# A two-layer streaming encoder on one core: stores of split weight tiles moved from the sync engine's queue to ScalarE's, with six edits of the step order around them

## The reference, cut to what matters

```python
def trunk(x, c, sample):
    for i in range(DEPTH):                                   # DEPTH = 2
        shift, scale, gate = modulation(c, ada_w[i], ada_b[i])        # silu(c) @ (1024 x 3072) + b
        h = rms_norm(x, norm_g[i]) * (1 + scale[:, None]) + shift[:, None]
        if i % 2 == 0:      # pool_mixer: u, gate = split(h @ w_in); trailing means of 2, 4, 8, 16 rows minus u;
            y, st = pool_mixer(h, hist, hist_pos, pool_w_in[j], pool_w_grp[j], pool_scale[j], pool_w_out[j])
        else:               # 16 heads on 4 key/value heads, chunk band of 3 x 64 keys, ALiBi, sink logits, silu gate
            y, kw, vw = attn_prompt(h, attn_w_in[j], attn_sinks[j], attn_w_out[j])   # attn_sample for the sample
        x = x + gate[:, None] * y
    return rms_norm(x, final_g), ...states
```

## Time and profile before

| what | us |
|---|---|
| runs, median (lowest to highest of 3) | 1622.16 (1614.68 to 1626.26) |
| profiled execution | 1625.29 |
| its span, first to last instruction | 1623.5 |
| TensorE busy in the span | 1565.5 |
| ScalarE busy in the span | 727.8 |
| mean granted TensorE clock | 0.984 of full |

### The profile page before, as it was taken

How to read it: one execution, slowest core, us unless ns; L and a number is a source line. 1 busy time by engine, 2 the same in 40 slices (tenths; PEclk the granted TensorE clock), 3 DMA queues, 4 the chain that set the end, 5 groups by cost and what they waited for, 6 DMA issues and landing times.

```text
span 1623.5 us, 26106 instructions
## 1 busy us (share of the span) xinstructions
PE 1565.5 (96%) x9211; PEld 1331.6 (82%) x9211; DVE 883.8 (54%) x2203; ACT 727.8 (45%) x1616; POOL 429.5 (26%) x403
## 2 busy tenths in 40 slices
PE   6899999999999999999999899999999999999997
PEld 4799988788878878788888898888788887888886
DVE  3465435563556455626666634666446664366652
ACT  3344433333332333225555554666435665456643
POOL 1233431211221212212222341333213333123332
PEclk9899999999999999999999999999999999999999
DMA  9688799996899699942233365334463334643323
GB/s 329 206 287 270 242 314 312 317 356 238 300 328 354 224 327 330 348 157 105 105 105 105 117 247 186 133 136 175 155 207 131 130 130 166 214 166 134 132 79 130
DMA packets 167855, 341.96 MB, mean 211 GB/s; under 512 B 22127, under 2 KB 84927, under 8 KB 167470
## 3 DMA queue, kind: packets, MB, share of 16 engines
q1 hardware_dynamic: 167726, 340.29, 60.0%
HBM read 266.13 MB, written 74.31 MB: 210 GB/s over the span
## 4 chain that ended last, share of the span: by engine, by line
PE 80%; DVE 6%; ACT 4%; issue 4%; DMA 2%; POOL 1%; SPq 0%; DVEq 0%; POOLq 0%; ACTq 0%
PE ps_u L1013 63%; PE ps_o L1258 4%; PE ps_s L1212 3%; PE ps_t L1231 3%; DMA work<-in_x_prompt_dram 1%; PE ps_s L1013 1%; DVE ps_u L1439 1%; PE ps_o L1057 1%; DMA w_raw<-in_pool_w_out_dram 1%; ACT ps_u L1760 1%; DVE work L1584 1%; DVE h_all_lo L1396 1%; ACT work L1865 1%; ACT sq L1806 1%; DVE silu_g L1468 1%
## 5 line engine op out<-in xcount | busy, mean ns | idle before, releaser
L1013 PE MATMUL ps_u<-h_all_hi,w_hi 128*128 128x512 f32 (+2 forms) x1440 | 520.6, 362 | 9.9 <-DVE h_all_lo L1396 2.9
L1013 PE MATMUL ps_u<-h_all_hi,w_lo 128*128 128x512 f32 (+2 forms) x1440 | 512.2, 356 | 0.0
L1013 PE MATMUL ps_u<-h_all_lo,w_hi 128*128 128x512 f32 (+2 forms) x1440 | 511.9, 355 | 0.0
L1013 PEld LDWEIGHTS ps_u<-h_all_hi,w_hi 128*128 128x128 f32 x1440 | 275.6, 191 | 55.4 <-DVE silu_g L1468 6.4
L1013 PEld LDWEIGHTS ps_u<-h_all_hi,w_lo 128*128 128x128 f32 x1440 | 275.9, 192 | 36.9
L1013 PEld LDWEIGHTS ps_u<-h_all_lo,w_hi 128*128 128x128 f32 x1440 | 276.0, 192 | 35.4
L2007 POOL TENSOR_TENSOR work<-work,recip 128x512 f32<-128x512 f32 (+2 forms) x136 | 133.0, 998 | 342.1 <-DVE recip L1601 340.6
L1013 PE MATMUL ps_u<-y_hi,w_hi 128*128 128x512 f32 (+1 forms) x584 | 214.6, 367 | 5.4 <-POOL y_lo L1986 5.3
L1439 DVE TENSOR_TENSOR ps_u<-ps_u,rstd_b 128x512 f32<-128x512 f32 (+1 forms) x180 | 107.1, 595 | 205.2 <-PE ps_u L1013 205.0
L1013 PE MATMUL ps_u<-y_hi,w_lo 128*128 128x512 f32 (+1 forms) x584 | 209.5, 359 | 0.0
L1013 PE MATMUL ps_u<-y_lo,w_hi 128*128 128x512 f32 (+1 forms) x584 | 209.2, 358 | 0.0
(11 more groups left out here) (240 smaller groups left out, 2321.5 us busy)
## 6 DMA issues: line engine op xcount, KB each, us to landing
w_hi<-w_hi_kept SPq DMA_DIRECT2D x176, 512.0 KB, 4.1
w_lo<-w_lo_kept SPq DMA_DIRECT2D x176, 512.0 KB, 5.4
chunks<-in_ada_w_dram SPq DMA_DIRECT2D x32, 512.0 KB, 6.3
w_hi_kept<-w_hi SPq DMA_DIRECT2D x28, 512.0 KB, 3.4
w_lo_kept<-w_lo SPq DMA_DIRECT2D x28, 512.0 KB, 4.8
w_hi_kept<-fore_hi SPq DMA_DIRECT2D x24, 512.0 KB, 6.4
w_lo_kept<-fore_raw SPq DMA_DIRECT2D x24, 512.0 KB, 7.8
opening<-in_ada_w_dram SPq DMA_DIRECT2D x16, 512.0 KB, 8.8
```

Source lines behind the costliest of these rows:

```text
L1013: last = nc.tensor.matmul(out, w, x, start=(i == 0), stop=(i == n - 1))
```

## The change

Seven edits, in the order of the steps:

1. The opening makes `h` in two halves. New steps `HF` make the second column block (272 columns) first; `W` 1 comes right behind them; `HS` of stage 0 makes the first block (272 columns) after the sums of squares. `XS` of x row tiles 0 and 1 moves up to their `XT`. The first two units wait for `HF` (new semaphores `h_first_hi`, `h_first_lo`), the third for `HS`.
2. GpSimd's `w_lo` of tile 2 waits until `SH` is done.
3. `XL` of the next part's row tiles 0 and 1 moves from the beginning of the output phase to before the last group's `z` units.
4. `MT` of modulation blocks 3 to 5 is cut into 6, 6 and 4 matmuls (`MP`, `MP`, `MT`), behind output tiles 5, 6 and 7 in place of all 16 behind tile 4.
5. In attention parts 1 to 3 the last item's `drain` moves from behind row block 6 of the first output unit to between row blocks 3 and 4 of the fourth.
6. In attention part 0 the first drained slot uses the ordinary order of its steps (softmax ahead of the low half of the turned weights).
7. `keep_tile` moves from the sync engine to ScalarE. ScalarE's step `W` of tile j, after its copy to `w_hi`, waits for both halves of tile j-1 and asks for its two stores; at the last tile of the stage it also waits for and stores that one.

```diff
             for t in range(n_tok):
                 s.append(("XT", 0, t))
+                if t < 2:
+                    s.append(("XS", 0, t))
                 if t == 1:
                     s.append(("MT", 0))
+            s.extend([("HF", k) for k in range(KT)])
+            self.split_to(1)
+            s.extend([("XS", 0, t) for t in range(2, n_tok)])
+            s.append(("NA", 0, 0))
             s.extend([("HS", 0, k) for k in range(KT)])
-            self.split_to(1)
-            s.extend([("XS", 0, t) for t in range(n_tok)])
-            s.append(("NA", 0, 0))
...
+            if g == GROUPS - 1 and p + 1 < PARTS:
+                s.extend([("XL", p + 1, 0), ("XL", p + 1, 1)])
             j = self.tile(("grp", g))
...
-            begin = [[("XL", p + 1, 0), ("XL", p + 1, 1)]]
+            begin = []
...
-            behind[4] = behind.get(4, []) + [("MT", 2 + p)] + ([("SH", 1)] if p == 2 else [])
+            m = 2 + p
+            behind[5] = behind.get(5, []) + [("MP", m, 0, 3)]
+            behind[6] = behind.get(6, []) + [("MP", m, 3, 6)]
+            behind[7] = behind.get(7, []) + [("MT", m)] + ([("SH", 1)] if p == 2 else [])
...
-        drain = [slot(a, drained=p == 0) for a in tail + [None, None, None]]
-        plan = [(0, 0, 6), drain[0], (1, 0, 6), drain[1], (2, 0, 6), drain[2], (3, 0, 6)]
+        drain = [slot(a, drained=p == 0 and a != tail[0]) for a in tail + [None, None, None]]
+        plan = [(0, 0, 6), drain[0], (1, 0, 6), drain[1], (2, 0, 6), drain[2]]
         if p == 0:
-            plan += [drain[3], (4, 0, 6)]
-        plan += [(0, 6, 7), drain[-1], (1, 6, 7), (2, 6, 7), (3, 6, 7)]
+            plan += [(3, 0, 6), drain[3], (4, 0, 6), (0, 6, 7), drain[-1]]
+        else:
+            plan += [(3, 0, 4), drain[-1], (3, 4, 6), (0, 6, 7)]
+        plan += [(1, 6, 7), (2, 6, 7), (3, 6, 7)]
...
                 elif st[0] == "W":
-                    keep_tile(st[1])
...
-                            if u["u"] not in stage_first:
+                            if u["u"] == 0:
+                                pe.wait_ge(h_first_hi, k + 1)
+                                pe.wait_ge(h_first_lo, k + 1)
+                            elif u["u"] not in stage_first and u["u"] != 2:
                                 pass
...
+                elif kind == "HF":
...
+                    for c, w, v in spans(COLS // 2, COLS // 2):
+                        last = V.scalar_tensor_tensor(out=h_lo[:, k, c:c + w], in0=x_even[:, k, c:c + w], scalar=gain[:, 0, k, v:v + 1],
+                                                      in1=h_hi[:, k, c:c + w].bitcast(F32), op0=ALU.mult, op1=ALU.subtract)
+                    last.then_inc(h_first_lo, 1)
...
         @block.scalar
         def _(act):
             A = nc.scalar.activation
+            owned = [st[1] for st in steps if st[0] == "W"]
+
+            def keep_tile(j):
+
+                act.wait_ge(w_hi_ready, splits(j))
+                act.wait_ge(w_lo_ready, splits(j))
+                n, i = width[j], kept.index(j)
+                act.dma_start(w_hi_dram[i, :, 0:n], w_hi[:, slot_of[j], 0:n].bitcast(F32)).then_inc(w_kept[slot_of[j]], 16)
+                act.dma_start(w_lo_dram[i, :, 0:n], w_lo[:, slot_of[j], 0:n].bitcast(F32)).then_inc(w_kept[slot_of[j]], 16)
...
                     A(w_hi[:, slot_of[j], 0:width[j]], w_raw[:, slot_of[j], 0:width[j]], ACT.Copy).then_inc(w_hi_ready, 1)
+                    if j - 1 in owned:
+                        keep_tile(j - 1)
+                    if j + 1 not in owned:
+                        keep_tile(j)
...
+                elif kind == "HF":
...
+                    for c, w, v in spans(COLS // 2, COLS // 2):
+                        last = A(h_hi[:, k, c:c + w], x_even[:, k, c:c + w], ACT.Copy, scale=gain[:, 0, k, v:v + 1])
+                    last.then_inc(h_first_hi, 1)
...
-                    for c, w, v in spans(0, cols(p)):
+                    for c, w, v in spans(0, cols(p) if stage else COLS // 2):
...
+                    if j == 2:
+                        pool.wait_ge(shift_ready, 1)
                     pool.wait_ge(w_hi_ready, splits(j))
```

More of the change, by code:

```diff
@@ L571, in trunk_kernel @@
         h_hi_ready, h_lo_ready = sem("h_hi_ready"), sem("h_lo_ready")
+        h_first_hi, h_first_lo = sem("h_first_hi"), sem("h_first_lo")
         ssum_done, var_ready, rstd_ready, diag_ready, rstd_spread, rb_ready = (
@@ L834, in load_tile @@
                 load_raw(t, w_raw[:, slot_of[j], :], raw_loaded[slot_of[j]])
[L836 to L842, removed]
             def fetch_tile(j):
@@ L912, in _ @@
                         load_ada(i + CHUNKS - 1)
-                elif st[0] == "W":
-                    keep_tile(st[1])
                 elif st[0] == "WL":
@@ L1047, in _ @@
                     last.then_inc(ada_done, 1)
-                elif kind == "MT":
+                elif kind in ("MP", "MT"):
                     m = st[1]
-                    if m >= 1:
+                    if kind == "MP" and st[2] == 0 or kind == "MT" and 1 <= m < 3:
                         claim("o", (mod_ready, m + 1))
@@ L1054, in _ @@
                         pe.wait_ge(ada_added, KT * (m + 1) - summed_from)
-                        for k in range(KT):
+                        for k in range(*st[2:4]) if kind == "MP" else range(6, KT):
                             for v in range(2):
@@ L1058, in _ @@
                                                         ones[:, 0:1], start=True, stop=True)
-                        last.then_inc(mod_turned, 1)
+                        if kind == "MT":
+                            last.then_inc(mod_turned, 1)
                         continue
@@ L1384, in _ @@
                         last.then_inc(x_put_dve, 1)
+                elif kind == "HF":
+                    k = st[1]
+                    dve.wait_ge(h_first_hi, k + 1)
+                    if k == 0:
+                        dve.wait_ge(x_put_dve, xt_dve[(0, TILES - 1)])
+                        dve.wait_ge(x_put_act, xt_act[(0, TILES)])
+                    for c, w, v in spans(COLS // 2, COLS // 2):
+                        last = V.scalar_tensor_tensor(out=h_lo[:, k, c:c + w], in0=x_even[:, k, c:c + w], scalar=gain[:, 0, k, v:v + 1],
+                                                      in1=h_hi[:, k, c:c + w].bitcast(F32), op0=ALU.mult, op1=ALU.subtract)
+                    last.then_inc(h_first_lo, 1)
                 elif kind == "HS":
@@ L1703, in _ @@
                     A(dump if p else row, row, ACT.Square, accum_out=ss[r0:P, t:t + 1]).then_inc(x_squared, 1)
+                elif kind == "HF":
+                    k = st[1]
+                    if k == 0:
+                        act.wait_ge(x_put_dve, xt_dve[(0, TILES - 1)])
+                        act.wait_ge(x_put_act, xt_act[(0, TILES)])
+                        act.wait_ge(mod_ready, 1)
+                    for c, w, v in spans(COLS // 2, COLS // 2):
+                        last = A(h_hi[:, k, c:c + w], x_even[:, k, c:c + w], ACT.Copy, scale=gain[:, 0, k, v:v + 1])
+                    last.then_inc(h_first_hi, 1)
                 elif kind == "HS":
```

## The result

| what | before | after |
|---|---|---|
| runs, median (lowest to highest) | 1622.09 (1614.68 to 1626.26, 4 runs) | 1597.24 (1596.11 to 1599.07, 4 runs) |
| profiled execution | 1625.29 | 1596.11 |
| its span | 1623.5 | 1594.3 |
| mean granted TensorE clock | 0.984 | 0.991 |

The changed kernel takes 0.9853 of the time of the kernel before (95% interval 0.9815 to 0.989). The forecast was 1600.

The account below looks back on a forecast made before the run. TensorE, busy 1565.5 of 1623.5 us, bounds the kernel, so only its idle time and low-clock stretches can give. Terms -5.9 - 4.9 - 9.7 - 4.9 + 1 = -24.4 from 1625.3 give 1600.9; forecast 1600, own range 1592 to 1607.

Parts of the forecast that it names:

- Edits 1 and 2 (-5.9): Opening: a smaller first `h` block and an undisturbed shift cast give 3.9 us, less low clock 2; together -5.9.
- near 48: Opening, sign to look for: the first 274-column unit starts near 48 us in place of 52.08.
- The term for the clock: Opening: with TensorE's wait cut to 0.7 us, 2 of the 5.1 us lost to low clock return; bounds 0 and 5.1.
- Edit 3 with the sync engine's share of edit 7 (-4.9): x row tiles near 211 us: loads asked for about 4 us sooner remove 3.3 us of waits and a 1.6 us fall.
- Rival (b): Opening and x loads: transfers hold them anyway, so the opening's low clock stays and x gains nothing; 1607 us, chance 0.15.
- Its second form: x loads: moving the stores doesn't free the sync engine, which now waits elsewhere; same 1607 us, within the same 0.15.
- The fall at 242: Low clock behind ten one-column sums: listed as costing 1.7 us, with no gain counted for it.
- Edit 4 (-9.7, one fall left): Modulation blocks: cutting them removes a 1.3 us wait and 10.1 us of low clock, less one 1.7 us fall.
- rival (a): Modulation blocks: the thin pieces keep the clock low, so cutting gives 1.2 us in place of 9.7; 1609 us, chance 0.20.
- Edit 5 (-4.9): Attention parts 1 to 3: the earlier drain removes three waits of 1.63 us on `y_lo`; -4.9.
- Edit 6 (0): Attention part 0: swapping two VectorE steps, bounds -0.5 and +0.5 us, taken as 0.
- Edit 7 on ScalarE (+1): First stage: 28 tiles' store pairs at 0.9 us each on ScalarE mostly fit its free time; +1 us, bounds 0 and +7.

Follow-up runs that it names:

- edit 7 alone: The kernel before with only the tile stores moved from the sync engine to ScalarE; 1614.46 us, ratio 0.9969.
- before + 2 + 4: The kernel before with only GpSimd's tile 2 split held until the shift is done and the modulation blocks cut; 1607.26 us, ratio 0.9923.
- after - 1 with the whole block: The changed kernel with the opening's two-half `h` undone and each modulation block's 16 matmuls uncut behind output tile 7; 1602.04 us, ratio 0.9884.
- stores not late: The changed kernel with GpSimd's tile 2 wait undone and ScalarE storing each tile in its own step from tile 3 on; 1619.34 us, ratio 0.9992.
- after again: The changed kernel unaltered, run and profiled a second time for its own spread; 1596.96 us, ratio 0.986.
- after - 1: The changed kernel with only the opening's two-half `h` undone, all 544 columns again made ahead of the first unit; 1600.38 us, ratio 0.9872.
- early fillers: The changed kernel with 33 more identity transposes, into a bank nothing reads, in TensorE's early opening waits; 1594.46 us, ratio 0.9847.

## Why the prediction was right, and which terms were not

**Edits 1 and 2 (-5.9): 6.2 and 8.3 measured.** Edit 2 did what its row said, the cast went from 2.24 to 0.17 us. The first 274-column unit starts at 48.80 in the execution that rose late, like the kernel before, and at 44.97 in the one that rose early; "near 48" was the former. Of the 52.08 - 48.80 = 3.3 us edit 2 brings 2.2 (it starts at 49.91 without edit 1) and edit 1 1.1, in place of the 2.1 and 1.8 counted. The term for the clock, 2 with bounds 0 to 5.1, measured 6.2 - 3.3 = 2.9. The step that failed is the reading of the earlier trace rows as one opening: when the clock rises, which none of the seven edits set, is worth 2.1 us with edit 1 (8.3 for 6.2) and 4.9 without it (8.0 for 3.1).

**Edit 3 with the sync engine's share of edit 7 (-4.9): right in sum, wrong in its owner.** The waits (2.7 and 0.6) and the fall of 1.6 went as worked out, but edit 7 alone does that, and edit 3 beside it nothing. The mechanism named the load of row tile 2, which edit 3 doesn't move; the chain said so, since its steps are the store's wait and the sync engine's order. The lead of "about 4 us" was 7.0. Rival (b), that transfers hold x anyway, is refuted: edit 7 alone gains the 6.0 with the stores still to be made and the load 1.7 us longer. Its second form, that the sync engine waits elsewhere, came true in the waits (156 us for 127) and not in its price, since this load was asked for 7.0 us sooner all the same.

**The fall at 242 (1.7), left out of the sum,** went as well: 2.7 + 1.6 + 1.7 = 6.0 is the whole stretch. Why is open: it stood in the kernel before, in before + 2 + 4 (230 to 238) and in after - 1 with the whole block (227 to 235), and in none of the other eleven profiles.

**Edit 4 (-9.7, one fall left): -11.4, the lower bound.** By its terms: 3.3 at 372, 1.6 at 532, 5.2 + 1.3 at 686, against 3.5, 1.5 and 6.4 alone on the kernel before. The one fall kept, taken from the ten sums at 239, was one too many; rival (a) falls with none in 30 cut blocks.

**Edit 5 (-4.9): 1.6 in each of the three parts, 4.7 to 4.8.** **Edit 6 (0):** not told apart; the stretch from 741 to 1001 spreads from +0.6 to -2.0 over the profiles, apart from the one with the stores not late, and falls there move from profile to profile with and without the edit.

**Edit 7 on ScalarE (+1): 0.0.** A pair was taken at 0.9 us and is 0.33 + 0.46 = 0.8, but in the changed kernel's timeline it runs beside ScalarE's ACTIVATEs, so nothing of it reaches the path. The argument that a wait there would pass through the banks to TensorE was sound, as the stores not late showed.

**The sum** was too small, and that it came near is in part luck. From the profiled execution 29.2 and 28.4 were gained against 24.4: edits 1 and 2, the fall at 242, edit 4 and edit 7 all gave more than was counted, and only the stretch from 741 to 1001 gave back (1.7 and 0.5). Against that stood the 3.1 allowed for that execution's standing above the median, and the first profile of the changed kernel stands 1.1 below its own. The medians differ by 24.9 where the forecast said 22.2.

## What to carry to other kernels

A transfer that waits for another engine should not stand in the queue that feeds the critical loads; put it on an engine that has the data anyway, late enough (here one tile) that its wait is over. One-column matmuls belong between full units in pieces, since a solid block of them brought TensorE's clock down for the units behind it in 11 of 12 places here, in three of them with TensorE never idle. And compare kernels stretch by stretch, at the same instruction: the column tells to 0.1 us what a median of runs that spread over 5 us can't, though only of the two executions compared, and one profile of the kernel before can be a slow one.

## What the runs showed of the hardware that was not expected

In the kernel before eight transposes at 25.59 took 1.95 us, as in "after again", while the granted clock of its windows read 1.00 from the start to 48 us; "after again" reads 0.57 for the same pace. A clock column of 1.00 at the beginning of a profile is no proof; the durations are. In after - 1, as in "after again" and before + 2 + 4, the clock was already up at 11 to 12 us (eight matmuls in 0.64 us in place of 1.08) and down again at the first transposes, behind a wait of 2.16 to 2.19 on x; with the early fillers that wait was 1.37 and the clock stayed up. And the issues on ScalarE's queue, 0.33 and 0.46 us, ran beside its ACTIVATEs: 56 of them in the first stage cost the path nothing. Where ScalarE had run dry behind a wait, as with the stores not late, the two were part of its idle time.
